# The first stage's input from a second, turned copy in memory, with dummy products and smaller first loads

## What is computed

```python
h = rms_norm(x, norm1_g[l])        # x * rsqrt(mean(x^2) + 1e-6) * g, per position
proj = h @ w_in[l]                 # 2048 -> 6160 columns
qa, ka, va, ra, ga, qb, kb, vb = jnp.split(proj, split_points, axis=-1)
...
qb = rms_norm(qb.reshape(Bsz, S, DIL_HEADS, DIL_DH), q_norm_g[l])
kb = rms_norm(kb.reshape(Bsz, S, DIL_HEADS, DIL_DH), k_norm_g[l])
```

## Time and profile before

| what | value |
|---|---|
| median of 3 runs | 1972.41 us (1971.65 to 1972.62) |
| the profiled execution | 1971.09 us |
| its span | 1969.3 us |
| PE busy | 1946.4 us, 99% |
| DVE, ACT, POOL busy | 1095.9, 939.1, 108.5 us |
| chain that ended last | PE 93%, DVE 3%, POOL 1%, ACT 1%, issue 1% |
| first DMA issued on SP | 0.75 us |

### The profile page before, as it was taken

The page is one execution under the profiler, slowest core; times in us unless marked ns, Lnnn a source line. Parts: engine busy times, 40 slices in busy tenths (PEclk is TensorE's granted clock), DMA queues, the critical chain, the costliest instruction groups (busy, mean ns, idle before and its releaser), DMA issues.

```text
span 1969.3 us, 22692 instructions
## 1 busy us (share of the span) xinstructions
PE 1946.4 (99%) x9062; PEld 1600.0 (81%) x9062; DVE 1095.9 (56%) x1330; ACT 939.1 (48%) x1230; POOL 108.5 (6%) x326
## 2 busy tenths in 40 slices
PE   8999999999999999999999999999999999999998
PEld 6788887788888888888888888888888888787787
DVE  4556455664545545445445556544655665666674
ACT  6445354554444344443444554444444464655653
POOL 1111000200000000000000010001100003001100
PEclk9999999999999999999999999999999999999999
DMA  7566564466665666665666566665566655544445
GB/s 238 175 193 171 152 173 159 154 179 192 186 192 190 193 193 190 187 189 193 193 190 191 182 193 183 192 193 171 168 184 189 192 179 176 150 150 141 138 149 161
DMA packets 182441, 352.74 MB, mean 179 GB/s; under 512 B 11136, under 2 KB 11952, under 8 KB 182336
## 3 DMA queue, kind: packets, MB, share of 16 engines
q1 hardware_dynamic: 181520, 349.18, 58.3%
q0 software_dynamic: 816, 2.11, 0.7%
HBM read 349.14 MB, written 2.11 MB: 178 GB/s over the span
## 4 chain that ended last, share of the span: by engine, by line
PE 93%; DVE 3%; POOL 1%; ACT 1%; issue 1%; DMA 0%; DVEq 0%; SPq 0%; ACTq 0%
PE g L790 29%; PE g L792 29%; PE g L791 29%; PE m L755 3%; DVE wl L1225 1%; ACT TW L985 1%; DVE st L1234 1%; PE m L871 1%; DVE TW L1225 1%; ACT wh L988 0%; POOL st L1589 0%; PE ob L889 0%; PE ob L888 0%; PE ob L887 0%; PE m L862 0%
## 5 line engine op out<-in xcount | busy, mean ns | idle before, releaser
L1225 DVE TENSOR_TENSOR wl<-raw,wh 128x1024 fp32r<-128x1024 f32 x657 | 801.5, 1222 | 770.7 <-ACT wh L988 770.1
L988 ACT ACTIVATE wh<-raw 128x1024 fp32r<-128x1024 f32 x657 | 694.5, 1058 | 837.6 <-PE g L792 834.9
L790 PE MATMUL g<-wh,xh 128*128 128x512 f32 x1888 | 748.0, 396 | 2.7 <-DVE wl L1225 2.7
L792 PE MATMUL g<-wh,xl 128*128 128x512 f32 x1888 | 736.8, 390 | 0.0
L791 PE MATMUL g<-wl,xh 128*128 128x512 f32 x1888 | 735.7, 390 | 0.0
L790 PEld LDWEIGHTS g<-wh,xh 128*128 128x128 f32 x1888 | 354.8, 188 | 80.1 <-issue 5.5
L792 PEld LDWEIGHTS g<-wh,xl 128*128 128x128 f32 x1888 | 354.6, 188 | 75.2
L791 PEld LDWEIGHTS g<-wl,xh 128*128 128x128 f32 x1888 | 355.1, 188 | 70.4
L790 PE MATMUL g<-wh,mh 128*128 128x512 f32 x736 | 291.5, 396 | 0.0
L792 PE MATMUL g<-wh,ml 128*128 128x512 f32 x736 | 287.1, 390 | 0.0
L791 PE MATMUL g<-wl,mh 128*128 128x512 f32 x736 | 286.7, 390 | 0.0
(11 more groups left out here) (131 smaller groups left out, 840.4 us busy)
## 6 DMA issues: line engine op xcount, KB each, us to landing
raw<-in_ev_w_in SPq DMA_DIRECT2D x128, 512.0 KB, 3.7
raw<-in_w_in SPq DMA_DIRECT2D x96, 512.0 KB, 3.9
raw<-in_w_gate SPq DMA_DIRECT2D x88, 512.0 KB, 4.3
raw<-in_w_up SPq DMA_DIRECT2D x88, 512.0 KB, 3.7
raw<-in_w_down SPq DMA_DIRECT2D x88, 512.0 KB, 4.7
raw<-in_od_w_in SPq DMA_DIRECT2D x72, 512.0 KB, 3.6
raw<-in_w_out SPq DMA_DIRECT2D x32, 512.0 KB, 4.3
raw<-in_ev_w_out SPq DMA_DIRECT2D x32, 512.0 KB, 3.7
```

The source lines that it names most:

```text
L790: e.matmul(o, hi[:, kt, c], h, start=first, stop=False)
L792: last = e.matmul(o, lo[:, kt, c], h, start=False, stop=end)
L988: return e.activation(o, i, AF.Copy, scale=scale)
L1225: return e.tensor_tensor(o, a, b, op)
```

## The change

A second copy of x, `xT`, with its features on the partitions, is prepared by the host and passed in beside x. It is loaded into the room of qT and kT, and ACT and DVE write xh and xl from it (`xsplit`), so PE has no transposes in stage 0. Block 0 has 9 units, since its first two are of one k-tile (256 KB) each; their loads are issued by ACT. DVE sets 512 columns of `wl` to a constant and PE runs nine dummy products on them into the bank m2. x in its natural layout, the rest of `small` and the tables for the bias are loaded later, behind units 6 to 12. The squares and the norm are said later, and the generators of `after` wait for the norm.

```diff
-XPARTS = ((0, 256), (256, 512), (512, 1024), (1024, 1536), (1536, 2048))
+XPARTS = ((0, 2), (2, 4), (4, 8), (8, 12), (12, 16))
         per = UW // b.n if b.n == 512 else len(b.kts)
-        for a in range(0, len(b.kts), per):
-            units.append(Unit(len(units), b, b.kts[a:a + per], a == 0, a + per >= len(b.kts)))
+        starts = [0, 1] if b.i == 0 else []
+        starts += range(per if starts else 0, len(b.kts), per)
+        for a, z in zip(starts, starts[1:] + [len(b.kts)]):
+            units.append(Unit(len(units), b, b.kts[a:z], a == 0, z == len(b.kts)))
             b.units.append(units[-1])
     return units
...
-        self.lanes["post"].append(self.first_acts())
-        self.step()
+        self.lanes["first"].append(self.first_acts())
+        say("warm")
         say("cut", 0)
         self.step()
         say("cut", 1)
+        self.step()
...
-            if b.n == 512:
+            if len(un.kts) == 2:
                 say("mul", u, 1)
             if un.end:
-                while b.acts[0] == "X" and self.norms < int(b.acts[1]) + 1:
+                while b.acts[0] == "X" and b.i and self.norms < int(b.acts[1]) + 1:
                     self.step()
                 self.launch("post", self.after(b))
...
     def first_acts(self):
         for kt in range(0, KT, 2):
-            self.say("xturn", "X0", kt)
-            if kt % 4 == 2:
-                self.say("sq", 0, kt // 4)
+            self.say("xsplit", "X0", kt)
+            yield
+        for j in range(4):
+            self.say("sq", 0, j)
+            yield
             yield
         self.say("norm", 0)
         self.lanes["att"].append(self.make_bias())
...
     def after(self, b):
         say, kind, a = self.say, b.done[0], b.done[1:]
+        while self.norms < 1:
+            yield
         if kind == "add":
             j, final, stage = a
             say("add", b.i)
...
-            on.wait_ge(s_id, 16)
             for p in plan.order:
                 kind, a = p[0], p[1:]
-                if kind == "mul":
+                if kind == "warm":
+                    on.wait_ge(s_warm, 1)
+                    for i in range(9):
+                        last = e.matmul(MB[2][:, :], wl[:, 2, 0:128], wl[:, 2, 0:512], start=True, stop=True)
+                    last.then_inc(s_warmed, 1)
+                elif kind == "mul":
                     u, half = a
                     un = units[u]
                     b = un.block
@@ -790,14 +820,11 @@
                             e.matmul(o, hi[:, kt, c], h, start=first, stop=False)
                             e.matmul(o, hi[:, kt, c], l, start=False, stop=False)
                             last = e.matmul(o, lo[:, kt, c], h, start=False, stop=end)
-                    if half == 1:
+                    if half == len(un.kts) - 1:
                         last.then_inc(s_mul, 1)
...
+            weights(e, 0).then_inc(s_raw[0], 16)
+            weights(e, 1).then_inc(s_raw[1], 16)
...
+                elif kind == "xsplit":
+                    kt = a[1]
+                    on.wait_ge(s_n1, 16)
+                    on.wait_ge(s_xt[[lo <= kt < hi for lo, hi in XPARTS].index(True)], 16)
+                    for i in range(2):
+                        last = copy(xh[:, kt + i, :], xT[:, kt + i, :], C("n1", kt + i, kt + i + 1))
                     last.then_inc(s_split, 1)
...
+                    if u == 2:
+                        on.wait_ge(s_warmed, 1)
                     tt(wl[:, u % NS, 0:m], raw[:, u % NR, 0:m], wh[:, u % NS, 0:m].bitcast(f32),
                        ALU.subtract).then_inc(s_lo, 1)
...
+                elif kind == "warm":
+                    e.memset(wl[:, 2, 0:512].bitcast(f32), 0.5).then_inc(s_warm, 1)
+                elif kind == "xsplit":
+                    kt = a[1]
+                    on.wait_ge(s_n1, 16)
+                    on.wait_ge(s_xt[[lo <= kt < hi for lo, hi in XPARTS].index(True)], 16)
+                    on.wait_ge(s_split, splits[p])
+                    for i in range(2):
+                        last = stt(xl[:, kt + i, :], xT[:, kt + i, :], C("n1", kt + i, kt + i + 1),
+                                   xh[:, kt + i, :].bitcast(f32), ALU.mult, ALU.subtract)
+                    last.then_inc(s_first, 1)
...
+                weights(e, u).then_inc(s_raw[u % NR], 16)
+
+            def turned_x(i):
+                k0, k1 = XPARTS[i]
+                e.dma_start(xT[:, k0:k1, :], t["xT"].rearrange("p (k t) -> p k t", k=KT)[:, k0:k1, :]
+                            ).then_inc(s_xt[i], 16)
+
+            n0, n1 = COLS["n1"]
+            e.dma_start(small[:, n0:n1], t["small"][:, n0:n1]).then_inc(s_n1, 16)
+            turned_x(0)
+            turned_x(1)
             load(2)
+            turned_x(2)
-            load_x(4)
             load(4)
             load(5)
...
                 kind, a = p[0], p[1:]
                 if kind == "cut" and a[0] >= LEAD and a[0] + NR < N:
-                    load(a[0] + NR)
+                    u = a[0] + NR
+                    load(u)
+                    if 6 <= u < 10:
+                        j = u - 6
+                        e.dma_start(x[:, :, 512 * j:512 * j + 512], t["x"].rearrange("(t p) d -> p t d", p=128)
+                                    [:, :, 512 * j:512 * j + 512]).then_inc(s_x[j], 16)
+                    elif u == 10:
+                        e.dma_start(rel, t["rel"]).then_inc(s_rel, 16)
+                        e.dma_start(oh, t["oh"]).then_inc(s_rel, 16)
+                        e.dma_start(lnn, t["lnn"]).then_inc(s_rel, 16)
+                        e.dma_start(w2[:, :], t["w2"]).then_inc(s_w2, 16)
+                        e.dma_start(small[:, 0:n0], t["small"][:, 0:n0]).then_inc(s_small, 16)
+                    elif u == 12:
+                        e.dma_start(small[:, n1:], t["small"][:, n1:]).then_inc(s_small, 16)
...
+    xT = np.asarray(x)[0].T.reshape(KT, 128, S).transpose(1, 0, 2).reshape(128, KT * S)
```

More of the change, by code:

```diff
@@ L118, in __init__ @@
         self.order, self.said, self.there, self.norms = [], set(), {}, 0
-        self.lanes = {"att": [], "fin": [], "post": []}
+        self.lanes = {"first": [], "att": [], "fin": [], "post": []}
         self.blocks, self.units = blocks, units
@@ L523, in program @@
                                             ("norm", "qk_sum", "g_sum", "r_sum", "on_sum"))}
-    splits = {p: n + 1 for n, p in enumerate(q for q in plan.order if q[0] in ("xturn", "mix", "cmix"))}
+    splits = {p: n + 1 for n, p in enumerate(q for q in plan.order if q[0] in ("xsplit", "xturn", "mix", "cmix"))}
     ropes = {p: n + 1 for n, p in enumerate(q for q in plan.order if q[0] in ("eq_rope", "on_rope"))}
@@ L563, in program @@
         s_raw = [sem(f"s_raw{i}") for i in range(NR)]
-        s_x = [sem(f"s_x{i}") for i in range(5)]
-        s_id, s_small, s_rel, s_w2, s_dec = sem("s_id"), sem("s_small"), sem("s_rel"), sem("s_w2"), sem("s_dec")
+        s_xt, s_x = [sem(f"s_xt{i}") for i in range(5)], [sem(f"s_x{i}") for i in range(4)]
+        s_first, s_warm, s_warmed = sem("s_first"), sem("s_warm"), sem("s_warmed")
+        s_n1, s_small, s_rel, s_w2, s_dec = sem("s_n1"), sem("s_small"), sem("s_rel"), sem("s_w2"), sem("s_dec")
         s_bw, s_br, s_out = sem("s_bw"), [sem("s_br0"), sem("s_br1")], sem("s_out")
@@ L626, in ready @@
                 p = plan.there[(acts, kt)]
-                key, n = ("conv", nth(*p)) if p[0] == "cmix" else ("bank", emptied[p][1])
+                if p[0] == "xsplit":
+                    key, n = "first", nth(*p)
+                else:
+                    key, n = ("conv", nth(*p)) if p[0] == "cmix" else ("bank", emptied[p][1])
                 out[key] = max(out.get(key, 0), n)
-            return [(s_cmix if key == "conv" else s_bank_dve, n) for key, n in out.items()]
+            by = {"first": s_first, "conv": s_cmix, "bank": s_bank_dve}
+            return [(by[key], n) for key, n in out.items()]
         def split_free(acts):
@@ L748, in aw_free, with weights @@
             return full(*before[-1]) if before else (s_bank, 0)
+        def weights(e, u):
+            un = units[u]
+            b, m = un.block, len(un.kts)
+            w = t[b.w]
+            if b.col is None:
+                src = w.rearrange("p (t n) -> p t n", n=b.n)
+            else:
+                r0 = b.row + 128 * un.kts[0]
+                src = w[r0:r0 + 128 * m, b.col:b.col + b.n].rearrange("(t p) n -> p t n", p=128)
+            return e.dma_start(raw[:, u % NR, 0:m * b.n].rearrange("p (t n) -> p t n", t=m), src)
         def tensor(e):
@@ L753, in four @@
             def four(dst, src):
+                on.wait_ge(s_small, 32)
                 for c in range(4):
@@ L1020, in scalar @@
                             last = copy(hi[:, kt + i, :], v[:, i, :], gain[i])
+                    last.then_inc(s_split, 1)
+                elif kind == "xsplit":
[4 more added lines that the diff above has]
```

(5 more changed lines are left out.)

58 lines of the change are left out of this document (16 added, 42 removed).

## The result

The changed kernel takes **1975.85 us** (median of 19 runs, 1974.54 to 1976.97), the kernel before 1972.21 (19 runs, 1971.46 to 1972.98): ratio 1.0019, 95% interval 1.0012 to 1.0025. It is slower by 3.6 us, just inside the 0.2% that the prediction called no change, and its interval leaves out 1. Forecast was 1975.0. The profiled execution took 1974.71 at a span of 1972.9, 3.6 above the old span.

A forecast was written before the change was run, and what follows sets the result against it. TensorE (PE) was taken as the bound, busy 1946.4 of 1969.3 us. Gains of 9.5 against losses of 11.8 to 12.5 gave net +2.3 to +3.0; the shift of +2.6 gave 1975.0 us, range 1970.8 to 1977.4.

The forecast's parts named there:

- The stall: PE waits some 9.8 us in front of q's first-half transposes, directly behind unit 16, until 61.3.
- The two roots: POOL's roots in the norm chain: first root to ACT's evacuation 4.07 us, second root 5.02 us.
- The beginning: Start of the kernel: first product moves from 8.76 to 6.3, unit 2 starts at 9.4.
- I take 4.1: Start of the kernel: n1, 256 KB of turned x and 256 KB of weights have landed at 4.1 us.
- With the earlier issue I take 7.1: Start of the kernel: unit 2's 512 KB of weights land at 7.1 us, where the old rates give 7.4.
- T: Start of unit 14, from which the norm chain is counted, forecast at 42.4 us.
- The clock behind the stall: PE runs at half pace behind the stall, with about 1 us for the rest of it among the products.
- The chain decides, not the clock: Next transposes behind the stall: the chain sets them at 77.05, PE itself arrives at 76.75; shift +2.6 us.
- The dummies: Nine dummy products at the beginning last to 5.3; units 0 and 1 taken at full pace behind them.
- the dummies do nothing: Rival, chance 0.12: first 2.7 us of products run at half pace, T is 1.0 later, total 1976.0 us.
- The later loads: Natural x (2 MB) and small (0.7 MB), queued after units 6 to 12, cost nothing.
- The faster rival: Rival, chance 0.06: the stall in front of q's transposes does not come, only gains are left, about 1965.5 us.

The follow-up runs named there:

- e1: Changed kernel with the squares at every multiplication, so the norm stands behind cut 12 in place of 16: 1968.89 us, ratio 0.9984 to the kernel before.
- e2: Changed kernel with the steps behind q's and k's blocks going on one per unit in the next block, not said at once: 1965.51 us, ratio 0.9967.
- e4: Kernel before with only the squares, norm and steps behind block 0 as late as in the changed kernel: 1979.98 us, ratio 1.0042.
- e7: e2's kernel with unit 1's weights loaded by SP behind the first part of turned x, not by ACT beside it: 1964.89 us, ratio 0.9964.
- e5: Changed kernel with 40 more dummy products in front of the transposes of q's first half: 1975.10 us, ratio 1.0015 to the kernel before.
- e9: Changed kernel with e2's and e1's edits and block 0's evacuation two steps behind the norm: 1961.92 us, ratio 0.9949 to the kernel before.
- e6: e2's kernel without the nine dummy products, their memset and the wait for them: 1966.19 us, ratio 0.9971 to the kernel before.
- e8: e2's kernel with 14 dummy products in place of 9: 1964.73 us, ratio 0.9963 to the kernel before.
- e13: e9's kernel with 14 dummy products in place of 9, loads as they were: 1962.91 us, ratio 0.9955 to the kernel before.
- e11: Kernel before with only the step order changed: e2's launch, block 0's evacuation two steps behind the norm, its transposes one unit later: 1966.01 us, ratio 0.9970.

## Why the prediction was right, point by point

- **The stall.** Right in place, cause and size: eight transposes directly behind unit 16, 9.56 us against 9.8, released by DVE's scaling. e1 and e2 take it away in two different ways, e4 makes it in the old kernel with 9.59, and the time follows each time.
- **The two roots.** 4.07 and 5.02 were worked out from what stands beside POOL on DVE; 4.02 and 5.01 came. The row of the bias addition was the one that decided the first.
- **The beginning.** This is where terms were mis-sized, two of them. "I take 4.1" for the landing of turned x: ACT could start on it only at 5.44, so the first product came at 7.53, not 6.3. "With the earlier issue I take 7.1" for unit 2's weights: ACT cut them at 8.22, so unit 2 came at 10.60, not 9.4, and T at 43.4, not 42.4. Both count the bytes as if they came strictly in the order in which they are needed. They don't: 0.62 MB had moved by 4.1, more than the 0.53 counted, and 2.0 MB by 8.22 (244 GB/s), not 1.57. e7 shows it for the first term, where without unit 1's weights beside it the start on x is at 4.33. It is the second term that moved T, for in e7 unit 2's weights are still cut at 8.26. The 1.0 us of T, with two differences of 0.2 behind it that cancel each other, makes up the 0.9 between the forecast shift of 2.6 and the measured one of 3.5 (74.45 to 77.95).
- **The clock behind the stall.** It fell as taken, to a granted 0.50. I had given it about 1 us of products; eight of them, 63.84 to 67.40, took 3.56 where 8 x 0.229 = 1.8 would do: 1.7 us. So PE reached the next transposes together with the chain (DVE's scaling began at 76.67, 1.28 in front of them) and did not wait. "The chain decides, not the clock" holds only just; e5, with the clock held, gained 0.75. The rule of the Trainium skill ("TensorE: Matmul & The Clock Gate", Part 1), that idleness takes the release back, agrees with the window at 0.50, which the trace of before could not show.
- **The dummies.** Taken to hold; they did in the profiled execution, where the gap behind them was 1.86. With gaps of 1.99 to 2.44 the profiles of e2, e1 and e5 show the pace low from the first product or from the second or third on, and so does e7's with a gap of only 0.75; e9's, with 1.64, shows full pace. The rival "the dummies do nothing" therefore holds in some executions and can be a part of the spread (2.4 us among the runs of the changed kernel, 1.5 among those of before); e6 bounds the worth of the nine at about 1 us; fourteen (e8) are 1.5 us better than none (e6), on the same chip.
- **The later loads**, priced at nothing. Right for the changed kernel, where ACT waited 2.02 for a load at 28.69 and PE never noticed; no longer free in e13, where the norm stands earlier and hangs on the same cuts.
- **The faster rival** had 1965.5 for the change without its stall; e2 came out at 1965.51. That the hundredths agree is luck: the rival had the first product at 6.3, full pace and old waits of 2.2; e2's profile has it at 7.66, half pace until 10.8 and waits of 3.3, and behind them one wait of 0.5 for DVE's scaling where the kernel before, and so the rival, has 2.7 us of them.

## What to carry to other kernels

A step that becomes cheap or is moved must be followed through everything that is queued behind it in order: here five microseconds had been saved at the beginning (the products of the old unit 7 start at 27.05 in place of 32.13) and a chain of seven handovers, 18.9 us long, was moved to where only 9 us of products stood beside it. Count, for every such chain, the work that the bound engine has between its start and the point where it needs the result, and where the order is written by a generator, look for the places where it says its rest at once. To start the first product earlier is worth no more than the loads of the next units allow.

## What the runs showed that I had not expected

- Idle times of nearly the same length left the clock in different states: after 2.11 us (e2, 56.05) products followed at full pace, after 2.43 us (e1, 45.77) at 0.43, with a granted clock of 1.00 and 0.53 in the stretches behind them; after gaps of 1.86 and 1.99 at the beginning, full and half pace, and half pace after one of only 0.75 (e7). The pace came back 3.0 us after the restart in e4 and 5.5 us after it in the changed kernel, behind the same eight transposes. A single profile of such a place is one draw.
- Eight transposes at the low level took 1.97, at the high one 1.09 (e5).
- The order of the steps alone (e11) gained 6.0 us, although the waits that it removed add up to 4.4. In the profiles 1.0 us of the rest is time in which PE was busy for less; the medians leave 0.7 that I can't place.
